# The entry of a two-layer decoder kernel: first modulation by column blocks of two feature tiles, three column slots multiplied tile by tile

## The reference, cut to what matters

```python
cond = jax.nn.silu(c)                                   # (1, 1024)
for l in range(2):
    mod = (cond @ w_mod[l] + b_mod[l])[:, None, :]      # 6 * 1024 columns
    sh1, sc1, g1, sh2, sc2, g2 = jnp.split(mod, 6, axis=-1)
    h = rms_norm(x, norm_gains[l, 0]) * (1.0 + sc1) + sh1
    y = token_mixer(h, w_in[l], ...)                    # below
    x = x + g1 * rms_norm(y, norm_gains[l, 1])
    h = rms_norm(x, norm_gains[l, 2]) * (1.0 + sc2) + sh2
    y = swiglu(h, w_gate_up[l], w_down[l])
    x = x + g2 * rms_norm(y, norm_gains[l, 3])

# token_mixer, its first lines
proj = h @ w_in
gq, gk, gv, gr, ga, dq, dk, dv = jnp.split(proj, IN_SPLITS, axis=-1)
log_a = jax.nn.log_sigmoid((ga @ w_gla_gate + b_gla_gate)) / 16
o_g = gla_chunked(gq, gk, gv, log_a)                    # gated linear attention, 4 heads
# then differential attention with a relative-position bias, 4 heads, and w_out
```

## Time and profile before

| | |
|---|---|
| median of 3 runs | 2387.83 us |
| lowest and highest | 2386.61 and 2388.2 us |
| profiled execution, span from first to last instruction | 2382.1 us |
| profiled execution, its own device time | not recorded beside the span; the median lies 5.7 us above the span |
| TensorE busy, share of the span | 2331.0 us, 98% |
| VectorE, ScalarE, GpSimd busy | 68%, 41%, 12% |
| mean granted TensorE clock | 0.994 of 2.4 GHz |
| bytes moved by DMA | 311.29 MB, mean 131 GB/s |

### The profile page before, as it was taken

How to read it: one execution, slowest core, us unless ns; L and a number is a source line. 1 busy time by engine, 2 the same in 40 slices (tenths; PEclk the granted TensorE clock), 3 DMA queues, 4 the chain that set the end, 5 groups by cost and what they waited for, 6 DMA issues and landing times.

```text
span 2382.1 us, 30623 instructions
## 1 busy us (share of the span) xinstructions
PE 2331.0 (98%) x11394; PEld 1882.1 (79%) x11394; DVE 1616.8 (68%) x2718; ACT 979.7 (41%) x1870; POOL 286.4 (12%) x356
## 2 busy tenths in 40 slices
PE   7999999999999999999999999999999999999997
PEld 5788767788788888888778887777888888888886
DVE  6765677757877777576762556776687777655767
ACT  6312455544333323344663125555443333324454
POOL 0416400011000000220120110000200000003001
PEclk9999999999999999999999999999999999999999
DMA  7956501132554554662331111102324554227434
GB/s 289 330 200 201 163 26 27 48 121 79 161 176 150 185 186 142 178 215 96 127 126 45 39 34 44 28 27 80 115 71 168 185 197 175 80 71 233 152 103 154
DMA packets 210755, 311.29 MB, mean 131 GB/s; under 512 B 13063, under 2 KB 145080, under 8 KB 206640
## 3 DMA queue, kind: packets, MB, share of 16 engines
q1 hardware_dynamic: 182688, 205.50, 26.4%
q0 software_dynamic: 27920, 103.84, 13.2%
HBM read 243.48 MB, written 71.02 MB: 132 GB/s over the span
## 4 chain that ended last, share of the span: by engine, by line
PE 91%; DVE 4%; issue 2%; ACT 1%; DMA 1%; POOL 0%; SPq 0%; ACTq 0%; DVEq 0%; POOLq 0%
PE ps L3063 32%; PE ps L3102 15%; PE ps L2593 9%; PE ps L2595 8%; PE ps L2594 8%; PE ps L2943 7%; PE ps L2889 3%; PE ps L2920 3%; PE ps L2908 1%; DVE ast L1932 1%; PE ps L2657 1%; PE ps L2871 1%; PE ps L2842 1%; PE ps L2864 1%; DMA mod_first<-in_w_mod 1%
## 5 line engine op out<-in xcount | busy, mean ns | idle before, releaser
L3063 PE MATMUL ps<-hT,wsp 128*128 128x512 f32 x1440 | 333.6, 389 | 2.6 <-issue 2.6
L3063 PEld LDWEIGHTS ps<-hT,wsp 128*128 128x128 f32 x1440 | 269.9, 188 | 60.0 <-issue 4.0
L2593 PE MATMUL ps<-hT,wsp 128*128 128x512 f32 (+1 forms) x744 | 308.2, 414 | 0.0
L2595 PE MATMUL ps<-hT,wsp 128*128 128x512 f32 (+1 forms) x744 | 290.6, 391 | 0.0
L2594 PE MATMUL ps<-hT,wsp 128*128 128x512 f32 (+1 forms) x744 | 289.6, 389 | 0.0
L3102 PE MATMUL ps<-wsp,asp 128*128 128x512 f32 x1056 | 249.7, 392 | 0.2
L3102 PEld LDWEIGHTS ps<-wsp,asp 128*128 128x128 f32 x1056 | 198.1, 188 | 44.0 <-issue 1.0
L3063 PE MATMUL ps<-tsum,wasp 128*128 128x512 f32 x960 | 226.4, 392 | 0.0
L3063 PEld LDWEIGHTS ps<-tsum,wasp 128*128 128x128 f32 x960 | 180.2, 188 | 39.6 <-DVE wasp L2388 0.4
L2593 PEld LDWEIGHTS ps<-hT,wsp 128*128 128x128 f32 x744 | 140.7, 189 | 30.9 <-issue 8.0
L2595 PEld LDWEIGHTS ps<-hT,wsp 128*128 128x128 f32 x744 | 140.3, 189 | 30.6
(11 more groups left out here) (296 smaller groups left out, 4270.9 us busy)
## 6 DMA issues: line engine op xcount, KB each, us to landing
F<-in_w_mod SPq DMA_DIRECT2D x80, 512.0 KB, 5.6
raw<-in_w_in SPq DMA_DIRECT2D x48, 512.0 KB, 3.8
raw<-in_w_gate_up SPq DMA_DIRECT2D x48, 512.0 KB, 4.9
raw<-sums_d SPq DMA_DIRECT2D x88, 256.0 KB, 3.0
F<-in_w_gate_up SPq DMA_DIRECT2D x40, 512.0 KB, 5.7
acts_d<-F POOLq DMA_DIRECT2D x38, 512.0 KB, 6.8
F<-acts_d POOLq DMA_DIRECT2D x76, 256.0 KB, 4.4
raw<-in_w_down SPq DMA_DIRECT2D x66, 256.0 KB, 3.9
```

What stands on the lines that cost most here:

```text
L2593: mm(o, a(0), b(0), start=start, stop=False)
L2595: return mm(o, a(1), b(0), start=False, stop=stop)
L3063: last = mm(bank(j, p), block_of(p, z)[:, k * P:k * P + P], times(p, zz, k), start=p < B_A22 and k == 0 and z == 0 and zz == 0, stop=k == ...
```

## The change: what it does

- **Order of loads.** The nine small tensors move from SP's queue to ScalarE's, so that SP issues constants, all of x, and then the modulation at once.
- **Column blocks.** `mod_first` and `first_chunk` go. The first modulation is loaded in four blocks q of two feature tiles: 256 columns of the shift and 256 of the scale, all eight input tiles, in four DMAs of 512 KB (rows of 1 KB) per block, laid where the two feature tiles of `hT` will be. Behind each block comes a piece of `w_in`: input tiles 2q and 2q+1 of the slots GQ1, GK0 and GK1 (384 columns). VectorE sums a block in eight products of 512 columns (`first_sums`), TensorE sums over the partitions (`first_mod_columns`), VectorE makes shift and scale of these two tiles alone (`first_columns`), ScalarE makes their high halves and the plain values in place (`first_hi`), VectorE the low halves. TensorE no longer multiplies modulation directly, and turns the tiles of x one after the other ahead of its first column sums.
- **Three slots tile by tile.** For each feature tile k TensorE multiplies GK0, GK1 and GQ1 into six PSUM banks: 12 matmuls that need only the high half of `hT`, then 6 that need the low half. The split weights of a tile lie in a ring of five (`stream_hi`, `stream_lo`). GA, GQ0 and WG follow as slots 3, 4 and 5.
- **Scaling of x.** VectorE scales all eight tiles; the four copies of the position bias now come before the means.
- **VectorE's list.** Shares 3 and 4 of the late modulation come around the split of `gaT`, then the low half of GV, then the gate bias (behind a wait for the gate product), share 5, the low half of GV+1, share 6, the log, share 7, and from there on as before. The exponential of the lambdas is made by ScalarE behind the first evictions, and VectorE waits for it ahead of the low half of GQ0.
- Two semaphores merge into others, and PSUM waits of the value slots follow the new banks.

```diff
 # SP
-            load_x(0)
-            load_x(1)
...
-            load_x(2)
-            load_x(3)
+            for i in range(4):
+                load_x(i)
             mods = w_mod.rearrange("l (k p) c -> p l k c", p=P)
-            for k in range(KT):
-                sp.dma_start(mod_first[:, k, :], mods[:, 0, k, 0:MOD1 * P]).then_inc(s_ml[k], 16)
-
+            firsts = w_mod.rearrange("l (k p) (z n) -> p l z k n", p=P, n=D)
+
+            def load_first(q, g):
+
+                for z in range(2):
+                    sp.dma_start(first_mods(q)[:, z, 4 * g:4 * g + 4, :],
+                                 firsts[:, 0, z, 4 * g:4 * g + 4, 2 * P * q:2 * P * q + 2 * P]
+                                 ).then_inc(s_ml[2 * q + g], 16)
...
+                def stream(q):
+
+                    sp.dma_start(k_raw(2 * q, 2).rearrange("p (k n) -> p k n", k=2),
+                                 win[:, 0, 2 * q:2 * q + 2, C_GQ + P:C_GQ + 4 * P]
+                                 ).then_inc(s_ml[first_weights(q)], 16)
+
                 if l == 0:
-                    sp.wait_ge(s_rbs, HEADS)
+                    for q in range(NQ):
+                        load_first(q, 0)
+                        load_first(q, 1)
+                        stream(q)
+                        if q == 0:
+                            sp.dma_start(raw_low0, win[:, 0, :, C_GA:C_GA + LOW]).then_inc(s_raw[1], 16)
+                    sp.wait_ge(s_rx, 6 + HEADS)
                     sp.dma_start(skew.rearrange("h q j -> q h j"),
...
+                    sp.wait_ge(s_kl, 4)
                     own_mods(range(MRING))
...
+                    sp.wait_ge(s_kl, KT)
+                    columns(N0_GQ, C_GQ)
+                    gate_weights(N0_WG)
+                    own_mods(ring_after(N0_WG))
 # ScalarE (behind its nine DMAs of the small tensors, the squares and Silu)
+                def stream_hi(k):
+
+                    i = first_weights(k // 2)
+                    act.wait_ge(s_ml[i], FIRST_IN[i])
+                    if k >= KRING:
+                        act.wait_ge(s_kp, k - KRING + 1)
+                    nc.scalar.activation(k_split(k, 0), k_raw(k), ACT.Copy).then_inc(s_kh, 1)
+
+                def first_hi(k):
+
+                    act.wait_ge(s_ab1, k // 2 + 1)
+                    a, b = cur[:, P_A + k:P_A + k + 1], cur[:, P_B + k:P_B + k + 1]
+                    nc.scalar.activation(hT[:, 0, k, :], x_turned[:, k, :], ACT.Identity,
+                                         scale=a, bias=b).then_inc(s_hh, 1)
+                    nc.scalar.activation(x_turned[:, k, :], x_turned[:, k, :], ACT.Identity,
+                                         scale=a, bias=b).then_inc(s_v, 1)
...
+                    for q in range(NQ):
+                        first_hi(2 * q)
+                        first_hi(2 * q + 1)
+                        if q + 1 < NQ:
+                            stream_hi(2 * q + 2)
+                            stream_hi(2 * q + 3)
+                    act.wait_ge(s_kp, KT)
+                    hi(l, N0_GQ)
...
+                    for b, dst in ((1, Fgk), (2, Fgk + S), (3, Fgq + S)):
+                        nc.scalar.activation(F[:, dst:dst + S], pair(b), ACT.Copy).then_inc(s_tev, 1)
+                    act.wait_ge(s_rx, 6)
+                    nc.scalar.activation(ast[:, 4:8], ast[:, 0:4], ACT.Exp).then_inc(s_cond, 1)
 # VectorE
+            for h in range(HEADS):
+                dve.wait_ge(s_rb, h + 2)
+                v.tensor_copy(bias_rows[:, 384 * h:384 * h + 384], ps[:, 2 + h, 0:384]
+                              ).then_inc(s_rx, 1)
+            for g in range(2):
+                first_mean(g)
+                dve.wait_ge(s_n1rs, g + 1)
+                for t in range(4 * g, 4 * g + 4):
...
+            first_sums(0, range(KT))
+            stream_lo(0)
+            stream_lo(1)
+            for q in range(NQ):
+                more = q + 1 < NQ
+                first_columns(q)
+                if more:
+                    first_sums(q + 1, range(0, 3) if q == 0 else range(2, 4))
+                if q == 0:
+                    lo_low(0)
+                first_lo(2 * q)
+                if more:
+                    first_sums(q + 1, range(3, 5) if q == 0 else range(4, 6))
+                first_lo(2 * q + 1)
+                if more:
+                    first_sums(q + 1, range(5, 8) if q == 0 else range(6, 8))
+                    stream_lo(2 * q + 2)
+                    stream_lo(2 * q + 3)
+                if q + 2 < NQ:
+                    first_sums(q + 2, range(0, 2))
+
+            dve.wait_ge(s_cond, 2)
...
-                lo(l, N_WG, 2 * LOW, 256)
+                if l == 0:
+                    lo(l, N0_GQ)
+                lo(l, N_WG if l else N0_WG, 2 * LOW, 256)
+                if l == 0:
+                    own_sums(3)
                 dve.wait_ge(s_gah, l + 1)
                 v.tensor_tensor(gaT[:, 1, :], pair(0)[0:2 * LOW], gaT[:, 0, :].bitcast(F32),
                                 ALU.subtract).then_inc(s_gal, 1)
-                lo_sums(N_GK0 + 2)
-                lo_sums(N_WG + 2)
+                if l == 0:
+                    own_sums(4)
+                    lo(l, N_GV)
+                    dve.wait_ge(s_pe, l * SLOTS + N0_WG + 1 + CREDIT)
...
-                lo_sums(N_GK1 + 2)
-                lo_sums(N_GQ0 + 2)
-                lo_sums(N_GQ1 + 2)
+                if l == 0:
+                    own_sums(5)
+                    lo(l, N_GV + 1)
+                    own_sums(6)
...
                                        W[:, 0:2048], ALU.min, ALU.subtract).then_inc(s_lg, 1)
+                own_sums(7)
                 lo_sums(N_GV + 2)
                 lo_sums(N_GV + 3)
 # GpSimd
-                pool.wait_ge(s_pe, l * SLOTS + N_WG + 1 + CREDIT)
+                pool.wait_ge(s_pe, l * SLOTS + (N_WG if l else N0_WG) + 1 + CREDIT)
 # TensorE
+                    first_mod_columns(0)
+                    pe.wait_ge(s_va, NT)
                     for k in range(KT):
+                        pe.wait_ge(s_kl, k + 1)
+                        pe.wait_ge(s_hh, k + 1)
+                        for o, w0, c0 in outputs:
+                            for z in range(2):
+                                mm(o, k_split(k, z)[:, w0:w0 + P], hT[:, 0, k, c0:c0 + HALF],
+                                   start=k == 0 and z == 0, stop=False)
+                        if k % 2 and k + 1 < KT:
+                            first_mod_columns(k // 2 + 1)
                         pe.wait_ge(s_hl, k + 1)
+                        for o, w0, c0 in outputs:
+                            last = mm(o, k_split(k, 0)[:, w0:w0 + P], hT[:, 1, k, c0:c0 + HALF],
+                                      start=False, stop=k == KT - 1)
+                        last.then_inc(s_kp, 1)
+                    split(N0_GA)
+                    low_columns((0, 1), range(KT)).then_inc(s_pe, 1)
+                    split(N0_GQ)
+                    pe.wait_ge(s_tev, 1)
+                    columns(N0_GQ % 2, 1).then_inc(s_pe, 1)
```

More of the change, by code:

```diff
@@ new lines, in _ @@
+            dve.wait_ge(s_cond, 2)
+            for l in range(L):
+                o = R_REST - P_GN
+                last = v.scalar_tensor_tensor(kept[:, l, o + P_LAM:o + P_LAM + 1],
+                                              ast[:, 4 + 2 * l + 1:4 + 2 * l + 2],
+                                              cst[:, C_LAM + 2 * l:C_LAM + 2 * l + 1],
+                                              ast[:, 4 + 2 * l:4 + 2 * l + 1], ALU.subtract, ALU.subtract)
+            last.then_inc(s_par, 1)
@@ L2739, in rows @@
                         split(n)
-                        for t in (2, 3, 4, 5, 6, 7, 0, 1) if i == 0 else range(NT):
+                        for t in (2, 3, 4, 5, 6, 7, 0, 1) if i == 0 and l else range(NT):
                             if i == 0:
```

345 lines of the change are left out of this document (182 added, 163 removed).

## The result

The changed kernel takes 2405.56 us (median of 4 runs, 2403.9 to 2406.12), the kernel before 2387.22 beside it: ratio 1.0077, 95% interval 1.0065 to 1.0089, so it is slower by some 18 us. The forecast was 2390.2 with 2378.5 to 2396.5; the time is outside.

The account below looks back on a forecast made before the run. TensorE, 98% busy, bounds the kernel; the first GLA step's start decides. VectorE's list consumes the 13.3 us head start: step at 152.9 against 150.55, +2.3 on 2382.1, plus 5.7 outside the span: 2390.2 us, range 2378.5 to 2396.5.

Parts of the forecast that it names:

- T: Landing time of the nine small loads on ScalarE's queue: taken as 7.5 us, bounds 6.5 to 13.9.
- step 2: Small loads and x: first four scalings done at 18.4 us, all at 22.5, last tile turned by 28.
- E: End of the streamed rounds of products: 72 us, between 69 and 76.
- step 6: VectorE's list from gate bias to second value copy: 58.7 us, putting the first GLA step at 152.9, +2.3.
- 1, loads: Start: first modulation block, with 1 KB rows, in at 19.7 to 22.3 us, bounded by 423 and 284 GB/s.
- rival B: Small loads land behind x, T 11.5 to 14, delaying VectorE's list: +4 to +6.5 more, near 2395; chance 0.2.
- step 3: First block of columns: VectorE's sum takes 6.2 us from 22.5, first large product at 32.0 against 47.66.
- 3 and 4, block and rounds: First column block, then four streamed rounds of 11.6, 10.8, 9.5 and 8.2 us, VectorE pacing them.
- Rival C: Rounds slower than VectorE's summed durations, through unoverlapped passes or 284 GB/s loads: E 77, +7.3, 2395; chance 0.11.
- 5: Rest of the columns: products of 20.9 us and a 0.7 wait, so value slots could start at 93.7.
- 7, the restart: TensorE restarting at half clock before the first GLA step: 0.5 us; behind it same instructions, nothing gained or lost.
- Rival A: TensorE keeps its head start: VectorE's list 48.7 us, GLA step at 142.4, -8, near 2380; chance 0.27.

Follow-up runs that it names:

- e1: Changed kernel with the nine small loads issued on SP's queue ahead of x: 2404.56 us, ratio 1.0072.
- e8: Changed kernel with e4's order, GpSimd's first two weight sums earlier, share 10 in halves from behind the value copies, small loads between x's halves: 2386.18 us.
- e12: Changed kernel with the edits of e2 and e5 together, so not all is computed: 2387.10 us, ratio 1.0006.
- e4: Changed kernel with shares 3, 4 and 5 of the late sum each one place forward in VectorE's list: 2397.01 us, ratio 1.0040.
- e2: Changed kernel with GpSimd's 12 operations of the first three weight sums left out of the computation: 2398.89 us, ratio 1.0048.
- e5: Changed kernel loading only a quarter of each late-modulation chunk, the rest of the sums of stale data: 2395.82 us, ratio 1.0037.
- e13: e11 with the edits of e2 and e5, so not all is computed: 2378.47 us, ratio 0.9969.
- e11: e8 with gaT's high half ahead of ScalarE's parameter-copy wait, and mean and scaling of tiles 0 to 3 before the small tensors: 2386.03 us.
- e14: e11 with the first two chunks of share 3 moved into the last round: 2385.94 us, ratio 1.0002.

## Why the prediction was wrong, step by step

Two terms of the sum failed: the landing T of the small loads in step 2 (7.5 taken, 13.4 measured), behind which the end of the rounds E came 5.5 us late, and the waits for chunks in step 6 (3.6 taken, 10.1 measured). The mechanism, VectorE's list behind the gate bias, was the forecast one.

**1, loads.** Right: the blocks came at 350 GB/s, in the bounds.

**2, small loads: wrong in size, in the direction of rival B.** T was taken as 7.5 and was 13.4, within the bound given. The rest of the step held: T + 10.9 = 24.3 for the first four scalings, measured 24.15. With T put in, the second four end at 28.4 (28.10), and step 3's 9.5 us give 37.9 for the first large product (37.32). What failed is the judgement that loads in a queue of their own pass those of x. The Trainium skill (DMA: Bandwidth & Descriptors, Queues, rings and completion order) says that each DMA engine takes the queues with work in turn, and by that rule I put T at the low end. The turns are in the trace: from 8 to 12 us SP's queue moved 270 packets and ScalarE's 256. The low end does not follow from them. Of the ScalarE queue's 460 packets 80 passed before 4 us, and 4, 96, 172, 84 and 24 in the stretches of 2 us from 4 to 14; the load that was waited for was the last issued (at 4.69) and the largest, 256 KB of the 0.4 MB. None of the three places tried is good: in front of x (e1) T was 9.5 and the first large product at 37.15, between its halves (e8, with other edits) 12.53 and 36.70. That the 5.9 us of T are what made E late is worked out from the sum above; no run has the small loads early and x on time.

**3 and 4, block and rounds.** Right: seven products of a block 5.54 us (forecast 0.75 and 0.07 between them, 5.7); rounds 40.2 us against 40. Rival C is not borne out.

**5.** Right: gate bias at E + 21.9, forecast E + 21.7.

**6, the list: right mechanism, its size 7.7 us short.** From gate bias to the second copy 66.4 us against 58.7. Operations as forecast (e12). Chunk waits 10.1, where I had 5.1 less 1.5 "as the ring of chunks is filled early": this is the term that failed, by 6.5 us. The first four chunks are early (issued at 45.5), but the ring's next loads wait until share 3 frees them, and share 3 stands behind the wait for the exponential: they are issued from 86.15 on, 13.3 us ahead of the gate bias, where it was 71.17 and 18.9 us before. That these 5.6 us less of lead made the 5.0 us of new waits fits e4, which takes share 3 ahead of that wait and has 6.1 behind the gate bias, but it is argued and not isolated. The queues were also fuller (a share of 0.95 from 99.4 to 150 us, before 0.87 from 90 to 150), and three single loads are 25.8 of the 90 us of the chain shown above. GpSimd's stretching is 10.1 against 8.4. The sum had spared operations of one input. The gate bias, which reads PSUM, was spared (2.73 us); the first products of a share were not: that at 102.05 took 2.74 us, where the one at 144.95 took 0.75, and three of them make 3.1 of the 10.1. e2 and e5 show each term, e12 their sum. The Trainium skill (GPSIMD Engine Reference, Specifications) has GpSimd's SBUF interfaces shared with VectorE. The runs agree: without GpSimd's operations e2's list is 7.9 us shorter.

**7, the restart.** 0.5 forecast. The first 14 products behind the wait took 5.8 us (166.05 to 171.87) instead of 3.2, most of them at 0.43 each as in the last row of the chain: 2.6.

The sum: E 5.5, gate bias 0.2, list 7.7, restart 2.1 are 15.5 on +2.3, so 17.8 of the 18.3 measured. The 5.7 us taken for what lies outside the span was not that: in later executions of the kernel before it is 1.8, so its profiled one was a quick one, by some 4 us; the difference of the two kernels does not change by it.

**Rival A** is refuted as stated: the list was not 48.7 but 66.4 us. Its price is not confirmed either. In e12 the list is 50.1 us up to the second copy and nothing is won, as the gate bias came at 98.2 and not at 93.7. In e13 the copies start 37.1 us behind the gate bias; that its 7.9 us are near rival A's 8 is chance. **Rival B** named T, and 5.5 of the 18 us go with it, by the sum.

## What to carry to other kernels

A head start for one engine is worth only what the in-order list of the next one allows: e8, e11 and e14 start TensorE 11 to 12 us earlier and win nothing, e13 with a shorter list wins 7.9. A ring that is filled early is not yet ahead: here its first four loads were issued at 45.5 us and the next at 86.15, when its first consumer had run, so look at what that consumer waits for. Take all disturbances of a list away at once, in one kernel that needn't compute, before you call a bound reached: e12 alone looked like the end.

## What the runs showed of the hardware that was not expected

- One-column operations of VectorE are held up by GpSimd as large ones are. In e8, beside GpSimd's two-input operations of 1.29 us, two such operations took 4.12 us; alone, in e13, they took 0.35.

```profile
89.19 4.12 DVE L1938 SCALAR_TENSOR_TENSOR kept<-ast,cst 128x1 f32<-128x1 f32 x2
```

- An operation of one SBUF input is held up too: `L1950`, 0.75 us alone, took 2.74 and 1.88 beside GpSimd in the changed kernel.
- Nine small loads (0.4 MB in all) in a queue of their own, issued by 5.06, had landed at 13.4; in the middle of the one queue with x they had landed at 11.53 and 12.53 (e8), in front of it at 9.50 (e1).
- Blocks with rows of 1 KB came at about 350 GB/s, rows of 8 KB at 423.
